# One table set for each root's logarithm and exponential, the first round's ids ahead of row pieces, and residuals ahead of the last tile's sums, in a two-layer decoder kernel

## The reference

```python
for layer in range(DEPTH):                       # 2
    hn = rmsnorm(h, norm_mix_w[layer])
    # layer 0: HGRN2 linear recurrence (4 heads) beside an S5 state space (32 groups)
    # layer 1: gated DeltaNet (8 heads), short causal convolutions on q, k and v
    h = h + mixed
    h = h + peer_ffn(rmsnorm(h, norm_ffn_w[layer]), ...)
return rmsnorm(h, norm_out_w)

def rmsnorm(x, w): return x * rsqrt(mean(x * x) + RMS_EPS) * w

def peer_ffn(xn, w_q, sub_keys, u_tab, v_tab):
    # q of 8 heads -> scores against 2 x 128 sub keys -> top 16 of each half
    # -> the 16 best of 256 pairs: expert_id, gate = softmax(sel_s)
    act = gelu(einsum('td,tkd->tk', xb, u_tab[eb]))      # 128 experts per token
    return einsum('tk,tkd->td', gb * act, v_tab[eb])
```

## Time and profile before

| | us |
|---|---|
| median of 3 runs (lowest, highest) | 3096.64 (3095.37, 3099.3) |
| the profiled execution, its own time | 3107.85 |
| its span | 3106.1 |
| busy: PE / DVE / ACT / POOL | 2128.0 / 2205.4 / 1466.2 / 1150.0 |
| first gather issued | 219.60 |
| moved by the gathers' queue | 1073.81 MB |

### The profile page before, as it was taken

One profiled execution on the slowest core, in us unless ns is written; L12 is line 12 of the kernel. 1 busy time (PEld: TensorE's weight loads), 2 busy tenths in 40 slices (PEclk: granted clock), 3 DMA queues, 4 the chain that ended last, 5 costly groups with the idle time before them and its releaser, 6 DMA issues.

```text
span 3106.1 us, 39537 instructions
## 1 busy us (share of the span) xinstructions
PE 2128.0 (69%) x13768; PEld 1273.4 (41%) x13768; DVE 2205.4 (71%) x6053; ACT 1466.2 (47%) x3475; POOL 1150.0 (37%) x1041
## 2 busy tenths in 40 slices
PE   7988888674456798877855898987665655453334
PEld 6776454350024575554522566655432411120001
DVE  8646888857777777867576757777866766767763
ACT  3424555433224756785433576778433422242222
POOL 0013334434444434434344333433444443443441
PEclk8889888785568799999877899999876866565555
DMA  5119999999999999989999999999999999999995
GB/s 216 69 57 390 419 419 419 405 378 421 421 420 415 416 392 393 412 318 411 418 420 421 403 362 411 391 412 372 421 420 421 420 421 421 421 421 422 421 421 234
DMA packets 182408, 1185.32 MB, mean 382 GB/s; under 512 B 19648, under 2 KB 25792, under 8 KB 50880
## 3 DMA queue, kind: packets, MB, share of 16 engines
q0 software_dynamic: 147456, 1073.81, 84.0%
q1 hardware_dynamic: 34752, 108.98, 9.1%
HBM read 1180.61 MB, written 2.10 MB: 381 GB/s over the span
## 4 chain that ended last, share of the span: by engine, by line
DMA 41%; PE 29%; ACT 10%; DVE 9%; issue 6%; POOL 4%; another core or an unknown queue 1%; ACTq 0%; SPq 0%; POOLq 0%; DVEq 0%
DMA arena<-uv_tab,cols 40%; PE ps L766 7%; PE xps L694 6%; POOL arena L651 4%; DVE arena L2192 4%; PE ps L694 4%; ACT scr L1433 2%; ACT L1433 2%; PE xps L1126 2%; ACT scr L1437 1%; PE xps L1200 1%; PE xps L1177 1%; PE ps L741 1%; PE xps L1197 1%; DVE arena L2275 1%
## 5 line engine op out<-in xcount | busy, mean ns | idle before, releaser
L651 POOL DMA_INDIRECT arena<-uv_tab,cols x1024 | 1145.9, 1119 | 1900.3 <-PE ps L766 1302.0
L2192 DVE CUSTOM_DVE_ANT_0 arena<-arena 128x1024 f32<-128x1024 f32 x1024 | 1250.6, 1223 | 627.0 <-DMA arena<-uv_tab,cols 598.3
L766 PE MATMUL ps<-arena,scr 128*32 128x512 f32 x4096 | 743.3, 804 | 715.9 <-ACT scr L1437 674.6
L1433 ACT ACTIVATE scr<-sel,cols 128x32 f32<-128x32 f32 x1024 | 273.3, 315 | 1109.6 <-DVE cols L2192 1073.1
L766 PEld LDWEIGHTS ps<-arena,scr 128*32 128x32 f32 x4096 | 93.0, 122 | 1077.0 <-ACT scr L1437 957.3
L694 PE MATMUL xps<-arena,wring 128*128 128x256 f32 x1600 | 394.2, 396 | 14.0 <-ACT arena L1639 5.7
L694 PEld LDWEIGHTS xps<-arena,wring 128*128 128x128 f32 x1600 | 304.8, 198 | 103.8 <-issue 43.7
L694 PE MATMUL ps<-arena,wring 128*128 128x256 f32 x1152 | 288.2, 407 | 4.8 <-DVE arena L1818 4.1
L1437 ACT ACTIVATE scr<-scr,cols 128x32 f32<-128x32 f32 x1024 | 273.0, 313 | 16.6
L694 PEld LDWEIGHTS ps<-arena,wring 128*128 128x128 f32 x1152 | 231.0, 205 | 87.3 <-issue 46.0
L1433 ACT ACT_TABLE_LOAD x158 | 202.7, 1283 | 2.8
(11 more groups left out here) (448 smaller groups left out, 2827.5 us busy)
## 6 DMA issues: line engine op xcount, KB each, us to landing
wring<-wall SPq DMA_DIRECT2D x176, 512.0 KB
arena<-uv_tab,cols POOLq DMA_INDIRECT x1024
arena<-wall SPq DMA_DIRECT2D x16, 512.0 KB, 7.3
h<-xT SPq DMA_DIRECT2D x2, 1024.0 KB, 11.4
arena<-glu_w SPq DMA_DIRECT2D x2, 1024.0 KB, 12.7
out<-arena SPq DMA_DIRECT2D x4, 512.0 KB
arena<-s_b SPq DMA_DIRECT2D x1, 512.0 KB, 8.9
arena<-s_bt SPq DMA_DIRECT2D x1, 512.0 KB, 9.6
```

Of the source, the lines that this page charges most:

```text
L651: pool.indirect_dma_start(out=whole_row(at), out_offset=None, in_=uv_tab, in_offset=bass.IndirectOffsetOnAxis(ap=ids[g % 2][:, k:k + 1], a ...
L766: mm = pe.matmul(ps[4 + half][32 * c:32 * c + 32, :], wdiag[:, b % PAIRS, j, :], pair_row(at + j, 1)[:, T * half:T * half + T], start=(g % ...
L1433: m = act.activation(wdiag[:, b % PAIRS, n % 2, :], place, ACT.Gelu, scale=dots[g % 2][:, n:n + 1])
L2192: dve.tensor_tensor_reduce(u, u, xrep[:, block_of(k), :], 1.0, 0.0, ALU.mult, ALU.add, dots[g % 2][:, k:k + 1]).then_inc(s["dot_done"], 1)
```

## The change

- At every root, a load of the set that has both functions is asked for ahead of the wait for the sum (in `finish` behind the wait for `side_mm`, since that wait stands at the function's top).
- TensorE: `across(0)` and `first_scores(1)` after pieces 0 and 1 instead of after 0 to 5. ScalarE: `soft(0)` ahead of `first_query(1)`, `first_scores(1)` after pieces 0 and 1. `two_heads` later on TensorE and closer together (3.25 instead of 0.5), a little earlier on ScalarE.
- `finish`: the residual matmuls of a half go ahead of its transposes. For the last tile both halves' residuals go ahead of the wait for `ycur`, half 1 into ps[0] instead of the side bank.
- The last tile is stored in two halves, the first as soon as VectorE has applied the root to four of the eight pieces.

```diff
+ROOT_SET = "natural_log_exp_and_others"
...
-            store(2 * TT - 1)
-            sp.wait_ge(s["out_stored"], 16 * TT)
+            for i in range(2):
+                sp.wait_ge(s[("half_normed", "tile_normed")[i]], (1, 2 * TT - 2)[i])
+                sp.dma_start(out[:, 4 * i:4 * i + 4, P * (TT - 1):P * TT],
+                             ysq[:, 4 * i:4 * i + 4, :]).then_inc(s["out_stored"], 16)
+            sp.wait_ge(s["out_stored"], 16 * (TT + 1))
...
             def finish(t, i):
 
-                side_free(("hy", t, i))
-                if i == 0:
-                    pe.wait_ge(s["y_copied"], t + 1)
+                last = t == 2 * TT - 1
+
+                def residual(i, o):
+
+                    for k in range(4 * i, 4 * i + 4):
+                        pe.matmul(o[:, tl(k % 4)], ident[:, :], h[:, k, tl(t % TT)], start=(k % 4 == 0), stop=False,
+                                  skip_group_check=True)
+
+                o = ps[0] if last and i == 1 else side
+                if not (last and i == 1):
+                    side_free(("hy", t, i))
                 if i < 2:
+                    if not (last and i == 1):
+                        residual(i, o)
+                    if last and i == 0:
+                        residual(1, ps[0])
+                    if i == 0:
+                        pe.wait_ge(s["y_copied"], t + 1)
                     for k in range(4 * i, 4 * i + 4):
-                        pe.matmul(side[:, tl(k % 4)], ycur[:, tl(k)], (ident[:, :], swap)[i], start=(k % 4 == 0), stop=False,
-                                  skip_group_check=True)
-                        mm = pe.matmul(side[:, tl(k % 4)], ident[:, :], h[:, k, tl(t % TT)], start=False,
+                        mm = pe.matmul(o[:, tl(k % 4)], ycur[:, tl(k)], (ident[:, :], swap)[i], start=False,
                                        stop=(k % 4 == 3), skip_group_check=True)
...
                         if hd + c:
-                            yield 1.5 * (2 * hd + c)
+                            yield 0.5 * (2 * hd + c)
...
-                yield 6.2
+                yield 3
...
-            paced += [Paced(-80, first_glu()), Paced(mixed_at(1) + 1, glu(1), g_slot(1)), Paced(0.5, two_heads())]
+            paced += [Paced(-80, first_glu()), Paced(mixed_at(1) + 1, glu(1), g_slot(1)), Paced(3.25, two_heads())]
...
-            for i in range(6):
+            for i in range(2):
                 first_tile_rows(i)
             across(0)
             first_scores(1)
-            for i in range(6, 8):
+            for i in range(2, 8):
                 first_tile_rows(i)
             first_sum(1)
...
             def norm_root(g):
 
+                act.preload_act_table_set(ROOT_SET)
                 act.wait_ge(s["sum_ready"], g + 1)
...
-                    src = side[:, :].rearrange("p (k t) -> p k t", k=4)
+                    src = (ps[0] if t == 2 * TT - 1 and i == 1 else side)[:, :].rearrange("p (k t) -> p k t", k=4)
...
                 else:
+                    act.preload_act_table_set(ROOT_SET)
                     if t >= 2:
...
                 yield 17
+                act.preload_act_table_set(ROOT_SET)
                 act.wait_ge(s["hg_sum"], n + 1)
...
+                act.preload_act_table_set(ROOT_SET)
                 act.wait_ge(s["hsum"], t + 1)
...
+                    act.preload_act_table_set(ROOT_SET)
                     act.wait_ge(s["l2_sum"], 2 * n + i + 1)
...
+                act.preload_act_table_set(ROOT_SET)
                 act.wait_ge(s["g_sum"], n + 1)
...
+                act.preload_act_table_set(ROOT_SET)
                 act.wait_ge(s["hsum"], gi + 2)
...
-            paced += [Paced(-81.5, first_glu()), Paced(mixed_at(1), glu(1), g_slot(1)), Paced(6, two_heads())]
+            paced += [Paced(-81.5, first_glu()), Paced(mixed_at(1), glu(1), g_slot(1)), Paced(5.25, two_heads())]
...
             first_scores(0)
+            soft(0)
             first_query(1)
-            for i in range(4):
+            for i in range(2):
                 first_tile_rows(i)
-            soft(0)
             first_scores(1)
-            for i in range(4, 8):
+            for i in range(2, 8):
                 first_tile_rows(i)
             first_norm(1)
...
                     m = norm_apply(n, root, src, dst, (2 * i, 2 * i + 1))
+                    if t == 2 * TT - 1 and i == 1:
+                        m.then_inc(s["half_normed"], 1)
```

More of the change, by code:

```diff
@@ L534, in trunk @@
             "y_copied", "tile_root",
-            "tile_normed", "small_loaded", "bc_loaded", "glu_loaded", "out_stored",
+            "tile_normed", "half_normed", "small_loaded", "bc_loaded", "glu_loaded", "out_stored",
             "const_pool", "masks_built", "sq_ready", "sum_ready", "root_ready", "hm_ready", "e_mm", "u_ready",
```

## The result

The changed kernel takes 3069.37 us (median of 4 runs, 3067.79 to 3076.64); the kernel before, measured beside it, 3096.01 us (4 runs, 3094.73 to 3099.3). The ratio is 0.9917, with a 95% interval of 0.9899 to 0.9935: 26.6 us faster, where 18.6 were forecast. The profiled execution took 3069.62 us by its own time, with a span of 3067.9, so this time the profile stands for the median; that of the kernel before did not (3107.85 against 3096.64). I cut the time as the prediction did.

The account below looks back on a forecast made before the run. The prediction took the gathers' DMA transfers to bound the stream, with gains only at holes, before the first gather and after the end. Its terms, 8.8 + 4.5 + 5.3 = 18.6 us off 3096.64, gave 3078 us, range 3063 to 3088.

Parts of the forecast that it names:

- four loads ahead of the first gather: Before the first gather: second table loads of the first norm, two heads and a 128-token norm go, 4 x 1.28 = 5.1 us.
- ids of round 0: Round 0's set-up: with `soft(0)` first and `across(0)` behind two pieces, the ids come at 215.4 instead of 219.14, 3.7 us.
- roots in the stream: Stream holes: eleven second loads on the chain give 14 us at the most; 4.5 us taken, between -3 and 14.
- end: After the last values: residuals ahead and an earlier clock rise give 4.3 us, the store in halves 1.0; together 5.3.
- rival of the closed holes: Stream: the lighter ScalarE closes holes at every load, 14 instead of 4.5 us, time 3068.5; chance 0.14.
- Start: Up to the first gather: loads and ids together bring it 5.1 + 3.7 = 8.8 us earlier, all carried.
- Late pieces: Under first gathers: 9.5 us of waits put down to the profiler, uncharged; rival, each piece costs 3.5 to 5.5 us, 3082, chance 0.18.
- the slower one: Under the first gathers: every moved piece is as late as the worst, 5.5 us, stream dry, time 3098.6; chance 0.04.
- Not carried: Early stream: held by something other than its start, so only 4.5 + 5.3 remain, time 3086.8; chance 0.05.
- not saved: Roots: the exponential still brings its own load, so only reorder (3.7) and end (5.3) remain, time 3087.6; chance 0.05.

Follow-up runs that it names:

- before, again: The kernel before with nothing edited, timed and profiled a second time: 3100.44 us against 3097.46, ratio 1.0008.

## Why the prediction was right in kind and 8 us too small

| term | forecast | measured |
|---|---|---|
| four loads ahead of the first gather | 5.1 | 5.2 timed; first search in the scores at 204.5 in the mean of the seven profiles with these loads, 199.4 in the six without |
| ids of round 0 | 3.7 | 4.0: from that search to the gather 15.00 before, 10.98 after |
| roots in the stream | 4.5 | 13.8 timed; stream 2856.0 (before, again) to 2842.2 |
| end | 5.3 | 3.6 timed; 5.3 in the profile against the first one of before |

**The step that failed** is the term "Roots in the stream": the mechanism was right and the size was not. The record had it in hand, eleven loads on the chain in the holes, 14 us at the most, and then cut it to a third, because most of the holes have other work on their chain too, TensorE's products above all. The runs don't bear out that discount. That TensorE is busy for 34.6 of 40 us says what other links the chain has, not that they would cover this one, and where the load went from the chain at 1364.60 nothing stepped in. The count was off as well: ten loads of roots go, while the record's eleven took in two that are none and left one out. Eleven times 1.28, 14.1, comes close to the measured 13.8 partly by luck; ten give 12.8. The rival of the closed holes, 3068.5 us, came within 0.9 us of the result, with the same luck. The bounds that the record gives for its three parts add up to 7 to 30 us, which is 3067 to 3090 us and not 3069 to 3086.

**Start.** Right in place and size, and carried. Between the means of the table lie 5.1 us, which are the four loads, and from the first search to the gather 3.8 to 4.0 us go. The order alone was timed at only 2.0 us, with an interval of zero to 5.6, which holds the 3.7 but doesn't show it; the start and the end together (13.7 of 14.1) do. By the Trainium skill (ScalarE: Activation LUTs, What ACT_TABLE_LOAD costs) a switch costs a drain besides the load, by its figures an estimated 10.6 us for the four. 5.2 were measured, with an interval up to 7.1, so what a second load costs here is the load's row alone.

**Late pieces.** The conclusion, to charge nothing, was right, and the reason given for it was wrong. I put the 9.5 us down to the profiler; the second profile of the same kernel doesn't have them. With this rival falls the slower one too, whose price came from the same two rows. The ninth gather comes 14.0 us after the first, where 16 were forecast; the DMA share of that stretch shows no gain by it.

**End.** The order of events came as written: residuals without a stop, the clock up before half 1 is transposed, the load as a swap at no gain, two stores. The two profiles differ by 17.23 - 13.01 = 4.2 us up to VectorE, 4.3 forecast, and 1.1 for the store, 1.0 forecast. But the old end itself has two lengths. In the second profile of before the clock rises before half 0 is through, and from the values to VectorE it takes 15.26 us; against that the new end of the changed kernel gains 2.3 and the store. The record's 5.3 was built on the longer of the two, but the new end varies as well. Over all profiles with a load between the sums and VectorE the old order takes 17.2 to 17.3 us in five and 15.2 to 15.4 in three, 16.5 in the mean, and the new one 13.01, 11.90 and 11.59, 12.2 in the mean: 4.3 less, as forecast. The timed 3.6 is the record's lower bound, with an interval of 1.2 to 6.8 that holds the 5.3.

**Not carried, not saved.** Both rivals fell: no load stands between logarithm and exponential (ScalarE has 46 loads fewer, 362 instead of 408), and the stream from the first gather on is as long with the early start as without it (2856.8 against 2856.0).

## What to carry to other kernels

The table loads that stood on the chain of waits inside the stream's holes counted whole here, 12.8 us by the count and 13.8 in the timed runs; sum those, and don't discount them for how busy the other engines are in the same window, nor multiply the saving over places that are not on the chain. Count them by the instruction that the edit touches, not by the shape of a line. Compare windows that start at the same event: a cut that starts 1.7 us later behind the first gather shows a share of 0.99 where the equal one has 0.95. Before a strange row gets an explanation, profile the same kernel a second time: an accident of one execution looks just like a mechanism. Where a load is asked for by hand, ask ahead of the last wait in front of the function, or a load that had been hidden comes into the open.

## What the runs showed of the hardware

- Two copies that start 4.3 and 5.3 us after their matmuls were seen in one profile of the kernel before and in none of the twelve others.
- TensorE's clock rises at different points of the same program: in the old order of the end one profile has 17.23 us from the last values to VectorE and another 15.26, and what differs on the timeline is the clock; in the new order it takes 13.01 in the changed kernel, and 11.90 in the kernel with the new end alone.
- The setup is no more even than that. With the second loads the first search in the scores came between 201.8 and 206.1 us in seven profiles, without them between 198.3 and 200.6 in six. A single pair of profiles gives the start to about 2 us.
